# Eight of eleven FFN down projections of a decoder layer as seven half-size products, with the gated rows kept in device memory

## Chip, cores and metric

One core of a Trainium2 chip runs one program. The metric is the device time in microseconds (us); lower is better. Engines: PE (TensorE matmul, PEld its weight load), DVE (VectorE), ACT (ScalarE), POOL (GpSimd), SP (SyncE, which issues the transfers).

## The reference, cut to what matters

One step of a hybrid decoder layer on 1024 prompt tokens and 32 new ones (1056 columns): a half-step SwiGLU FFN, a mixer with attention and convolution, a cross-attention, and a second half-step FFN. The change concerns only the two FFNs:

```
def swiglu_ffn(x, g, w_gate, w_up, w_down):
    h = rmsnorm(x, g)
    return (jax.nn.silu(h @ w_gate) * (h @ w_up)) @ w_down
...
xp = xp + 0.5 * swiglu_ffn(xp, ffn1_norm[l], ffn1_w_gate[l], ffn1_w_up[l], ffn1_w_down[l])
```

D_MODEL is 1024, D_FF 2816, everything is float32.

## The kernel before

The tokens lie along the free dimension. T = 1056 columns; halves HW = 528, quarters QW = 264, thirds TT = 352. The residual stream `x_res` (8 blocks of 128 features by 1056) stays in SBUF. Every float32 product is three matmuls: high weight by high operand, high by low, low by high, where the high part is a rounded copy (ACT writes it) and the low part what remains (POOL for weights, DVE for operands).

`SevenFFN` computes one FFN. The 2816 hidden features are 22 chunks of 128, two chunks to a group, 11 groups. Group 0 (`plain`) multiplies directly. In each of the groups 1 to 10 a chunk's gate and up products are made by a seven-product scheme: seven "units" (gate1, gate2, T3, T2, T1, T4, up2), each 2 x 4 x 3 = 24 matmuls of 264 columns, so 168 matmuls to a chunk. The weight sums T1 to T4 are made on POOL (`summed`), the high parts on ACT (`sum_high`, `direct_high`), the low parts on POOL (`weight_low`), in six rotating buffers ("homes"). DVE evicts (`evict`), ACT does SiLU. The gated rows go to `f_ghi` and `f_glo`, and the group's down projection follows at once: 24 tiles (8 feature blocks by 3 thirds), each 2 chunks x 3 = 6 matmuls of 352 columns (lines 1271, 1275, 1276), each tile added to `x_res` by one DVE instruction (line 1553). Groups 2 to 9 are a hardware loop.

Every engine has its own in-order list. PE's `free` names what must be read before a PSUM bank is written again. In the last group DVE has more to do: in FFN1 (`nth == 0`) each add is followed by the low part of the next norm's operand (line 746), and `closing` on DVE releases PE's next product; in FFN2 ACT squares and scales each added tile and DVE sums the squares (line 714, and line 1588 for the last six tiles, one after the other), before the final normalisation and output.

Of the kernel before, what the change touches and what calls it, by code (L numbers as in the profile page):

```python
# [25 lines left out]
P = 128  # L26
# [49 lines left out]
FF_UNITS = 18 * (FF_CHUNKS // 2)  # L76
FF_LEAD = 6
FF_LOADS = 3 * (FF_CHUNKS // 2)
# [85 lines left out]
def hybrid_layer(nc, a, o):  # L164

    ctx = ExitStack()
    with ctx:
# [69 lines left out]
        for n, name in enumerate(("A22", "A11", "S3", "A21", "A12", "S1", "S2")):  # L237
# [16 lines left out]
                     rs=f_rs[:, :].rearrange("p (a b) -> p a b", a=NTT))  # L254
        conv_w0 = at("conv_w0", [P, 4, CONV_WIDTH], f_g_off + 16 * T + 12 * QW)
# [773 lines left out]
        class SevenFFN:  # L1029
# [24 lines left out]
            N_EV, N_ACT, N_MM = len(EVENTS), len(ACTS), 14  # L1054

# [9 lines left out]
            EV0, ACT0, MM0 = PLAIN_EV - 2 * N_EV, PLAIN_ACT - 2 * N_ACT, PLAIN_MM - 2 * N_MM  # L1065
            TOTAL_EV, TOTAL_ACT, TOTAL_MM = 2 * GROUPS * N_EV + EV0, 2 * GROUPS * N_ACT + ACT0, 2 * GROUPS * N_MM + MM0
# [28 lines left out]
            def done(self):  # L1095
                return self.tile_added(self.GROUPS - 1, self.N_TILES - 1)

            def event(self, g, c, name):
                return self.evicted, self.nth * self.TOTAL_EV + self.EV0 + self.N_EV * (2 * g + c) + self.EVENTS.index(name) + 1

            def act_done(self, g, c, name):
                return self.acted, self.nth * self.TOTAL_ACT + self.ACT0 + self.N_ACT * (2 * g + c) + self.ACTS.index(name) + 1
# [4 lines left out]
            def low_done(self, g, c, unit):  # L1107
                return past(self.low, self.UNITS * g + 7 * c + self.LOW_AT[unit])

            def high_done(self, g, c, unit):  # L1110
                return past(self.high, self.UNITS * g + 7 * c + self.HIGH_AT[unit])

            def sum_done(self, g, c, unit):
                return self.summed, 8 * (self.GROUPS - 1) * self.nth + 8 * (g - 1) + 4 * c + self.SUM_AT[unit]

            def down_unit(self, view, g, n):
                return past(view, self.UNITS * g + 15 + n)

            def tile_added(self, g, i):
                return self.added, self.N_TILES * (self.GROUPS * self.nth + g) + i + 1  # L1120

            def tile_done(self, g, i):
                return self.down_done, self.N_TILES * (self.GROUPS * self.nth + g) + i + 1

            def raw_landed(self, slot, g, n):
                return w_landed[slot], 16 * (self.landed0 + 3 * g + n + 1)

            def home_free(self, eng, g, n):

                eng.wait_ge(*past(self.used, self.UNITS * g + n - 4))  # L1130

            @staticmethod
            def home(c, unit):
                return (7 * c + unit) % HOMES
# [6 lines left out]
            def groups(self, eng, plain, group):  # L1141
# [16 lines left out]
            def loads(self, sp):  # L1158
# [5 lines left out]

                def group(g, first, last):
                    for c in range(2):
                        sp.wait_ge(*(self.sum_done(g, 0, self.W_T4) if c else self.down_unit(self.low, g - 1, 1)))
                        self.gate_load(sp, 2 * g + c)
                        sp.wait_ge(*(self.low_done(g, 0, self.UP2) if c else self.down_unit(self.low, g - 1, 3)))
                        self.up_load(sp, 2 * g + c)  # L1170
# [4 lines left out]
                self.groups(sp, plain, group)  # L1175
# [23 lines left out]
            def pe(self, pe, opening, closing=None):  # L1199
# [4 lines left out]
                def chunk(g, c, first):  # L1204
                    def free(unit, s):
                        if unit == self.GATE1:
                            return self.event(g, 0, "up_first%d" % s) if c else self.tile_added(g - 1, 18 + s)
# [2504 lines left out]
```

## Time and profile before

| | |
|---|---|
| median of 3 runs | 2503.03 us (2502.71 to 2507.26) |
| profiled execution: span, first to last instruction | 2501.9 us |
| what lies around the span (median less span) | 1.1 us |
| PE busy | 2448.5 us, 98% |
| DVE, POOL, ACT busy | 1348.7, 936.2, 911.0 us |
| DMA | 185.73 MB, mean 74 GB/s |

No time of its own is listed for the profiled execution beside its span. Busy is the share of time in which an engine had an instruction under way; matmuls overlap, so the sum of their durations is more than PE's busy time, and the distance from one to the next says what one costs.

### The profile page before, as it was taken

The page shows a single profiled execution, that of the slowest core. Times are in us where ns is not written, and L with a number is a line of the kernel's source. Part 1 is how long each engine was busy: PE and PEld are TensorE (multiplying, and loading weights), DVE is VectorE, ACT ScalarE, POOL GpSimd, SP SyncE. Part 2 cuts the span into 40 slices and gives each one's busy share as a digit, 9 for nine tenths or more (in the row PEclk, how much of TensorE's full clock was granted, in tenths as well). Part 3 has the DMA queues.
Part 4 walks back from the last instruction along what each step waited for, and adds up shares of the span by engine and source line. Part 5 has one row for each costly group of instructions (what it writes and reads, how often), then busy time and mean ns, then how long its engine had stood idle before and what let it go on. Part 6 is the DMA issues. An engine that isn't in the chain of part 4 may idle for free.

```text
span 2501.9 us, 47597 instructions
## 1 busy us (share of the span) xinstructions
PE 2448.5 (98%) x18207; PEld 2300.7 (92%) x18207; DVE 1348.7 (54%) x2603; ACT 911.0 (36%) x2042; POOL 936.2 (37%) x709
## 2 busy tenths in 40 slices
PE   7999999999999999998999999999999999999998
PEld 7999999999999998666777999789999999999998
DVE  6644444444474556765777761444654444444446
ACT  7333333333241334555443330332433233333326
POOL 2755555555543250002120222013465555555551
PEclk9999999999999999999999999999999999999999
DMA  3111111111123122006563312331111111111112
GB/s 124 34 52 51 50 50 50 50 50 50 51 70 117 49 67 80 1 1 261 186 230 127 130 42 74 130 126 43 43 52 52 51 50 48 45 46 46 50 51 87
DMA packets 175514, 185.73 MB, mean 74 GB/s; under 512 B 8360, under 2 KB 151049, under 8 KB 172566
## 3 DMA queue, kind: packets, MB, share of 16 engines
q1 hardware_dynamic: 171263, 144.55, 18.7%
q0 software_dynamic: 3584, 37.75, 3.8%
q8 instruction: 88, 1.44, 0.2%
q10 hardware_dynamic: 543, 1.69, 0.2%
q14 instruction: 36, 0.29, 0.0%
HBM read 167.66 MB, written 12.52 MB: 72 GB/s over the span
## 4 chain that ended last, share of the span: by engine, by line
PE 63%; ACT 3%; DVE 1%; issue 1%; ACTq 0%; DVEq 0%
PE ps L1236 5%; PE ps L1231 5%; PE ps L1235 5%; PE ps L397 5%; PE ps L400 5%; PE ps L401 5%; PE ps L1276 3%; PE ps L1275 3%; PE ps L1271 3%; PE ps L2352 2%; PE ps L2322 2%; PE ps L2367 1%; PE ps L2334 1%; PE ps L2533 1%; PE ps L2463 1%; PE ps L2664 1%
## 5 line engine op out<-in xcount | busy, mean ns | idle before, releaser
L1231 PE MATMUL ps<-op_hi_S,home_hi 128*128 128x264 f32 x1280 | 364.5, 285 | 0.0
L1235 PE MATMUL ps<-op_lo_S,home_hi 128*128 128x264 f32 x1280 | 364.0, 284 | 0.0
L1236 PE MATMUL ps<-op_hi_S,home_lo 128*128 128x264 f32 x1280 | 363.9, 284 | 0.0
L1553 DVE SCALAR_TENSOR_TENSOR x_res<-ps,x_res 128x352 f32<-128x352 f32 x528 | 270.4, 521 | 168.7 <-PE ps L1276 168.5
L1276 PE MATMUL ps<-f_ghi,home_lo 128*128 128x352 f32 x1056 | 340.8, 323 | 0.0
L1275 PE MATMUL ps<-f_glo,home_hi 128*128 128x352 f32 x1056 | 339.9, 322 | 0.0
L1271 PE MATMUL ps<-f_ghi,home_hi 128*128 128x352 f32 x1056 | 339.4, 321 | 0.4 <-DVE f_glo L1512 0.4
L1512 DVE TENSOR_TENSOR ps<-f_copy,ps 128x264 f32<-128x264 f32 x160 | 70.0, 438 | 456.5 <-PE ps L1236 456.5
L1231 PE MATMUL ps<-op_hi_A,home_hi 128*128 128x264 f32 x960 | 273.5, 285 | 0.0
L1236 PE MATMUL ps<-op_hi_A,home_lo 128*128 128x264 f32 x960 | 273.1, 284 | 0.0
L1235 PE MATMUL ps<-op_lo_A,home_hi 128*128 128x264 f32 x960 | 272.8, 284 | 0.0
L1236 PEld LDWEIGHTS ps<-op_hi_S,home_lo 128*128 128x128 f32 x1280 | 241.1, 188 | 0.0
L1235 PEld LDWEIGHTS ps<-op_lo_S,home_hi 128*128 128x128 f32 x1280 | 241.1, 188 | 0.0
L1231 PEld LDWEIGHTS ps<-op_hi_S,home_hi 128*128 128x128 f32 x1280 | 240.3, 188 | 0.0
L397 PE MATMUL ps<-h_hi,w_hi 128*128 128x352 f32 x696 | 229.5, 330 | 5.5 <-DVEq L3188 2.9
L1598 POOL TENSOR_TENSOR home_lo<-home_v,home_hi 128x512 fp32r<-128x512 f32 x160 | 205.2, 1293 | 68.3 <-ACT home_hi L1319 68.3
L400 PE MATMUL ps<-h_lo,w_hi 128*128 128x352 f32 x696 | 225.3, 324 | 0.0
L401 PE MATMUL ps<-h_hi,w_lo 128*128 128x352 f32 x696 | 225.2, 324 | 0.0
L2011 POOL CAST w_hi<-w_raw 128x1024 fp32r<-128x1024 f32 x40 | 41.9, 1048 | 484.6 <-PE ps L397 174.9
L1319 ACT ACTIVATE home_hi<-home_v 128x512 fp32r<-128x512 f32 x160 | 100.8, 630 | 310.9 <-POOL home_v L1611 309.6
L1598 POOL TENSOR_TENSOR home_lo<-f_raw,home_hi 128x512 fp32r<-128x512 f32 x120 | 156.7, 1320 | 124.9 <-ACT home_hi L1319 124.9
L1271 PEld LDWEIGHTS ps<-f_ghi,home_hi 128*128 128x128 f32 x1056 | 198.5, 188 | 0.9 <-DVE f_glo L1512 0.9
(394 smaller groups left out, 5698.6 us busy)
## 6 DMA issues: line engine op xcount, KB each, us to landing
f_raw<-in_ffn_w_gate SPq DMA_DIRECT2D x44, 512.0 KB, 3.8
f_raw<-in_ffn_w_up SPq DMA_DIRECT2D x44, 512.0 KB, 3.8
f_raw<-in_ffn_w_down SPq DMA_DIRECT2D x44, 512.0 KB, 3.7
ring<-in_cache_mem_k SPq DMA_DIRECT2D x16, 512.0 KB, 3.7
ring<-in_cache_mem_v SPq DMA_DIRECT2D x16, 512.0 KB, 5.0
w_raw<-in_w_in SPq DMA_DIRECT2D x14, 512.0 KB, 3.9
x_keep<-x_res SPq DMA_DIRECT2D x1, 4224.0 KB, 18.0
x_res<-x_keep SPq DMA_DIRECT2D x2, 2112.0 KB, 8.2
```

Source lines behind the costliest of these rows:

```text
L397: mm = pe.matmul(out, w_hi[:, slot, c0:c0 + m], hi, start=start, stop=False)
L400: pe.matmul(out, w_hi[:, slot, c0:c0 + m], lo, start=False, stop=False)
L401: return pe.matmul(out, w_lo[:, slot, c0:c0 + m], hi, start=False, stop=stop)
L1231: mm = pe.matmul(out, w, xhi[:, k, q], start=self.STARTS[unit] and k == 0, stop=False, skip_group_check=True)
L1235: pe.matmul(out, w, xlo[:, k, q], start=False, stop=False, skip_group_check=True)
L1236: mm = pe.matmul(out, lo, xhi[:, k, q], start=False, stop=self.STOPS[unit] and k == KH - 1, skip_group_check=True)
L1271: mm = pe.matmul(out, whi, f_ghi[:, c, cols], start=(c == 0), stop=False)
L1275: pe.matmul(out, whi, f_glo[:, c, cols], start=False, stop=False)
L1276: mm = pe.matmul(out, wlo, f_ghi[:, c, cols], start=False, stop=(c == 1))
L1319: act.activation(home_hi[h][:, :], src[:, :], ACT.Copy).then_inc(self.high[0], 1)
L1553: dve.scalar_tensor_tensor(out=x, in0=ps[:, bank, 0:TT], scalar=0.5, in1=x, op0=ALU.mult, op1=ALU.add).then_inc(self.added, 1)
L1598: pool.tensor_tensor(home_lo[h][:, :], src[:, :], home_hi[h][:, :].bitcast(F32), ALU.subtract).then_inc(self.low[0], 1)
```

## The change

Groups 0, 1 and 10 keep their direct down projection; group 10's now comes at the very end. Groups 2 to 9 are "staged": gate and up as before, but the gated rows are not projected. DVE writes them into a buffer `st` and forms four sums of 528 columns (S3 after the first chunk; S1, S2, S4 after the second, all three in a row), and SP stores 2 and then 5 planes of 528 columns to the device memory tensor `g_keep`. There are seven homes while groups are staged.

After group 10's gate and up, four "spans" run, each for two staged groups (K: two chunks each; tokens: two halves). A span has seven products; a product is 8 tiles of 264 columns (4 feature blocks by 2 quarters), each 2 x 3 = 6 matmuls: 336 matmuls. Its operands are read back from `g_keep` (seven transfers), split by ACT (`operand_high`) and DVE (`operand_low`, both inputs in SBUF); the 14 weight blocks, 8 of them sums, are made as before on POOL and ACT. DVE adds each tile to a running sum in SBUF (`span_sum`) or straight to `x_res`. After the last span POOL forms U2, U3, U4, V (16 additions of 528 columns, `combine`) and DVE adds them to `x_res` in 16 additions of 528 columns (`half_added`, both inputs in SBUF), twelve of them ahead of the tiles of group 10's down projection.

```
-FF_UNITS = 18 * (FF_CHUNKS // 2)
+STAGED = (2, FF_CHUNKS // 2 - 1)
+SPANS = 4
...
+        st = at("st", [P, 5, HW], f_g_off)
+        st_copy = at("st_copy", [P, 2, QW], f_g_off + 20 * HW)
...
+        g_keep = nc.dram_tensor("g_keep", (P, FF_CHUNKS // 2, 7, HW), F32, kind="Internal").ap()
...
                 plain()
                 group(1, True, False)
-                with eng.Fori(2, self.GROUPS - 1) as g:
-                    group(g, False, False)
-                group(self.GROUPS - 1, False, True)
+                with eng.Fori(*STAGED) as g:
+                    staged(g)
+                group(self.LAST, False, True)
+                if span is None:
+                    return
+                span(0)
+                with eng.Fori(1, SPANS - 1) as q:
+                    span(q)
+                span(SPANS - 1)
...
+                def staged(g):          # on SP
+                    chunk_after(g, 0, 2 * g + 1)
+                    sp.wait_ge(*self.event(g, 0, "S3"))
+                    sp.wait_ge(const_in, 32)
+                    sp.dma_start(g_keep[:, bass.ds(g, 1), 0:2, :], st[:, 1:3, :].unsqueeze(1)).then_inc(self.stored, 16)
+                    chunk_after(g, 1, 2 * g + 2)
+                    sp.wait_ge(*self.event(g, 1, "S4"))
+                    sp.wait_ge(const_in, 32)
+                    sp.dma_start(g_keep[:, bass.ds(g, 1), 2:7, :], st[:, :, :].unsqueeze(1)).then_inc(self.stored, 16)
...
                 def group(g, first, last):   # on ACT
+                    if last:
+                        act.wait_ge(*self.all_stored())
                     chunk(g, 0, first, last)
                     chunk(g, 1, first, last)
...
+                    for p in range(7):       # span, on PE
+                        pe.wait_ge(*self.operand_at(self.operand_low, q, p))
+                        for j in range(8):
+                            mb, cols = j // 2, slice(j % 2 * QW, (j % 2 + 1) * QW)
+                            out = ps[:, self.SPAN_BANKS[j], 0:QW]
+                            pe.wait_ge(*bank_free(p, j))
+                            for i in range(2):
+                                m = 2 * p + i
+                                if j == 0:
+                                    pe.wait_ge(*self.span_low(q, m))
+                                whi, wlo = (x[m % 7][:, mb * P:(mb + 1) * P] for x in (span_hi, span_lo))
+                                xhi, xlo = (x[p][:, i, cols] for x in (g_hi, g_lo))
+                                mm = pe.matmul(out, whi, xhi, start=(i == 0), stop=False)
...
+                                pe.matmul(out, whi, xlo, start=False, stop=False)
+                                mm = pe.matmul(out, wlo, xhi, start=False, stop=(i == 1))
...
+                def operand_low(q, p):   # on DVE
+                    dve.wait_ge(*self.operand_at(self.operand_split, q, p))
+                    dve.tensor_tensor(g_lo[p][:, :, :], g_v[p][:, :, :], g_hi[p][:, :, :].bitcast(F32),
+                                      ALU.subtract).then_inc(self.operand_low, 1)
...
+                    if c == 0:               # staged_end, on DVE
+                        evict("S3", st[:, 2, :], st[:, 1, :], st[:, 0, :], ALU.subtract, self.event(g, 0, "gated_first1"))
+                    else:
+                        evict("S1", st[:, 0, :], st[:, 0, :], st[:, 2, :], ALU.add, self.event(g, 1, "gated_first1"))
+                        evict("S2", st[:, 1, :], st[:, 1, :], st[:, 0, :], ALU.subtract, self.event(g, 1, "S1"))
+                        evict("S4", st[:, 4, :], st[:, 3, :], st[:, 1, :], ALU.add, self.event(g, 1, "S2"))
...
+                def plane_recombined(mb):
+                    if mb < 4:
+                        half_added(block_of(mb, 1), span_sum[3][mb][:, :], self.combined("U3", mb), self.span_tile(self.added, SPANS - 1, 3, 7))
+                        dve.wait_ge(*self.recombined(4 + mb))
+                    else:
+                        half_added(block_of(mb, 0), span_sum[0][mb - 4][:, :], self.combined("U4", mb - 4),
+                                   self.span_tile(self.added, SPANS - 1, 6, 7))
+                        half_added(block_of(mb, 1), span_sum[1][mb - 4][:, :], self.combined("V", mb - 4))
+                        dve.wait_ge(*self.recombined(8 + 2 * (mb - 4) + 1))
...
                 def down_add(g, i, mb, tt, bank):
+                    if g == self.LAST and tt == 0:
+                        plane_recombined(mb)
                     dve.wait_ge(*self.tile_done(g, i))
```

The words "on SP", "on ACT", "on PE" and "on DVE" behind some lines are added here. `span_free` lets the buffer of weight block m be written once PE has begun block m - 5, which for the odd block of product p is the start of product p - 2.

## Rows read from the trace of the kernel before

**Rows 1.** The page: busy time of each engine, and the granted clock.
```profile
PE 2448.5 (98%) x18207; PEld 2300.7 (92%) x18207; DVE 1348.7 (54%) x2603; ACT 911.0 (36%) x2042; POOL 936.2 (37%) x709
...
PEclk9999999999999999999999999999999999999999
```

**Rows 2.** Groups of PE by shape, and one FFN1 group as a window.
```profile
L1231 PE MATMUL ps<-op_hi_S,home_hi 128*128 128x264 f32 x1280 | 364.5, 285 | 0.0
...
L1276 PE MATMUL ps<-f_ghi,home_lo 128*128 128x352 f32 x1056 | 340.8, 323 | 0.0
...
200.70:264.60 63.90, 63.90 (x482) 63.90 (x481) 29.62 (x69) 19.82 (x46) 33.25 (x26) 1.00 0.17 50
```

**Rows 3.** Timeline of DVE: start, us, instruction; the first eviction of three chunks.
```profile
169.16 0.44 DVE L1512 TENSOR_TENSOR ps<-f_copy,ps 128x264 f32<-128x264 f32 x1 [4.08 <-PE ps L1236]
...
170.94 0.77 DVE L1512 TENSOR_TENSOR ps<-ps,f_rs 128x264 f32<-128x264 f32 x2
...
189.56 0.44 DVE L1512 TENSOR_TENSOR ps<-f_copy,ps 128x264 f32<-128x264 f32 x1 [2.54 <-PE ps L1236]
...
233.04 0.44 DVE L1512 TENSOR_TENSOR ps<-f_copy,ps 128x264 f32<-128x264 f32 x1 [4.05 <-PE ps L1236]
```

**Rows 4.** Timelines of POOL, ACT and DVE around a second chunk's start.
```profile
249.18 1.30 POOL L1611 TENSOR_TENSOR home_v<-f_raw 128x512 f32<-128x512 f32 x1
...
253.21 1.29 POOL L1598 TENSOR_TENSOR home_lo<-home_v,home_hi 128x512 fp32r<-128x512 f32 x1
...
251.90 0.63 ACT L1319 ACTIVATE home_hi<-home_v 128x512 fp32r<-128x512 f32 x1 [0.76 <-POOL home_v L1611]
...
248.91 0.44 DVE L1512 TENSOR_TENSOR ps<-ps,f_rs 128x264 f32<-128x264 f32 x1
```

**Rows 5.** Instructions on `op_v_S` (min/median/max ns), two timeline rows, one DVE group.
```profile
L836 DVE SCALAR_TENSOR_TENSOR op_v_S<-x_res,gains,op_v_S x32: 755/1421/1864, 47.8 to 1829.2; 128x528 f32<-128x528 f32 x32
...
L857 POOL TENSOR_TENSOR op_lo_S<-op_v_S,op_hi_S x24: 1322/1334/1806, 59.8 to 1831.8; 128x528 fp32r<-128x528 f32 x24
...
59.54 6.04 DVE L836 SCALAR_TENSOR_TENSOR op_v_S<-x_res,gains,op_v_S 128x528 f32<-128x528 f32 x4
...
59.77 7.00 POOL L857 TENSOR_TENSOR op_lo_S<-op_v_S,op_hi_S 128x528 fp32r<-128x528 f32 x4 [1.86 <-ACT op_hi_S L833]
...
L1512 DVE TENSOR_TENSOR f_glo<-ps,f_ghi 128x264 fp32r<-128x264 f32 x64 | 24.6, 426 | 2.1
```

**Rows 6.** Transfers: issues, KB each, us from issue to landing.
```profile
x_keep<-x_res SPq DMA_DIRECT2D x1, 4224.0 KB, 18.0
...
out<-kv_stage SPq DMA_DIRECT2D x1, 1024.0 KB, 5.1
```

**Rows 7.** Timelines of DVE and PE at the end of FFN1, and a window.
```profile
719.45 1.48 DVE L1553 SCALAR_TENSOR_TENSOR x_res<-ps,x_res 128x352 f32<-128x352 f32 x3 [0.84 <-PE ps L1276]
...
730.87 0.51 DVE L1553 SCALAR_TENSOR_TENSOR x_res<-ps,x_res 128x352 f32<-128x352 f32 x1
731.31 0.57 DVE L746 SCALAR_TENSOR_TENSOR h_lo<-x_res,gains,h_hi 128x352 fp32r<-128x352 f32 x1
731.80 0.51 DVE L1553 SCALAR_TENSOR_TENSOR x_res<-ps,x_res 128x352 f32<-128x352 f32 x1
...
736.33 2.28 DVE L746 SCALAR_TENSOR_TENSOR h_lo<-x_res,gains,h_hi 128x352 fp32r<-128x352 f32 x1
...
742.91 0.40 PE L397 MATMUL ps<-h_hi,w_hi 128*128 128x352 f32 x1 [2.91 <-DVEq L3188]
...
743.64:747.05 3.41, 3.41 (x13) 3.41 (x13) 3.41 (x2) 0.90 (x3) 3.33 (x2) 0.51 1.04 280
```

**Rows 8.** Timelines of DVE and ACT at the end of FFN2.
```profile
2460.10 1.39 DVE L1553 SCALAR_TENSOR_TENSOR x_res<-ps,x_res 128x352 f32<-128x352 f32 x3
...
2462.83 1.37 DVE L1553 SCALAR_TENSOR_TENSOR x_res<-ps,x_res 128x352 f32<-128x352 f32 x3
...
2482.61 0.53 DVE L1588 TENSOR_TENSOR acc_end<-acc_end,sq_end 128x352 f32<-128x352 f32 x1 [0.69 <-ACT sq_end L1451]
```

More of the change, by code:

```diff
@@ L1177, in plain_products, with span_low, span_high, span_free @@
+                self.groups(sp, plain, group, staged)
+                for q in range(SPANS):
+                    span(q)
+            def span_low(self, q, m):
+                return past(self.low, self.span_unit(q) + m + 1)
+            def span_high(self, q, m):
+                return past(self.high, self.span_unit(q) + m + 1)
+            def span_free(self, eng, q, m):
+                eng.wait_ge(*past(self.used, self.span_unit(q) + m - 4))
             def plain_products(self, pe, c, u, q, free=None, planes=range(KH), starts_unit=False):
@@ L1649, in group, with staged, span_low @@
                     chunk(g, 1)
-                    for n in range(4):
-                        down_low(g, n)
                     if not last:
+                        for n in range(4):
+                            down_low(g, n)
                         ahead(g + 1, 0)
-                self.groups(pool, plain, group)
+                def staged(g):
+                    chunk(g, 0)
+                    ahead(g, 1)
+                    chunk(g, 1)
+                    ahead(g + 1, 0)
+                def span_low(q, m):
+                    name, i = self.SPAN_WEIGHTS[m // 2], m % 2
+                    src = span_v[m % 7][:, :] if name[0] == "T" else block(i, name)
+                    pool.wait_ge(*self.span_high(q, m))
+                    pool.tensor_tensor(span_lo[m % 7][:, :], src, span_hi[m % 7][:, :].bitcast(F32), ALU.subtract).then_inc(self.low[0], 1)
@@ new lines, in block, with span_sum_of @@
+                def block(i, name):
+                    r, h = int(name[1]) - 1, int(name[2]) - 1
+                    return span_raw[i][:, r, 512 * h:512 * h + 512]
+                def span_sum_of(q, i, name, a, b, op, *waits):
+                    m = 2 * self.SPAN_WEIGHTS.index(name) + i
+                    for known, value in waits:
+                        pool.wait_ge(known, value)
+                    self.span_free(pool, q, m)
+                    pool.tensor_tensor(span_v[m % 7][:, :], a, b, op).then_inc(self.summed, 1)
@@ new lines, in combine @@
+                def combine(name, mb, out, a, b, *waits):
+                    for known, value in waits:
+                        pool.wait_ge(known, value)
+                    pool.tensor_tensor(span_sum[out][mb][:, :], span_sum[a][mb][:, :], span_sum[b][mb][:, :], ALU.add).then_inc(self.summed, 1)
+                self.groups(pool, plain, group, staged, span)
+                at = [self.span_tile(self.added, SPANS - 1, p, 7) for p in range(7)]
+                for mb in range(4):
+                    combine("U2", mb, 2, 2, 0, at[2])
@@ L1879, in _ @@
                 if m < 2:
-                    sp.wait_ge(w_used, U_WIN - 4 + m)
-                    sp.wait_ge(*ffn1.down_unit(ffn1.low, ffn1.GROUPS - 1, 1 + 2 * m))
+                    sp.wait_ge(w_used, U_WIN - 3)
+                    sp.wait_ge(*ffn1.down_unit(ffn1.low, ffn1.LAST, 1 + 2 * m))
                 else:
```

420 lines of the change are left out of this document (360 added, 60 removed).

## The prediction

> **What bounds the kernel now.** I read the page first: PE is busy 98% of the span, at full granted clock in all slices, while DVE, ACT and POOL are busy 36 to 54% [rows 1]. In one FFN1 group (window) PE is busy in all 63.90 us, DVE in 29.6 and POOL in 33.3 [rows 2]. So what the groups cost is what PE issues. The durations of matmuls overlap, so I take the price of one from distances. Between the first evictions of a group's two chunks lie 20.40 us, and between those of two groups 63.88 us [rows 3]. A chunk is 168 matmuls of 264 columns: 121.4 ns each. Two chunks leave 23.08 us for the down projection, 144 matmuls of 352 columns: 160.3 ns each. PE waits for nobody inside a group. The exceptions are the two ends. At the end of FFN1 PE sits idle 2.91 us until DVE releases it, and then runs 3.41 us at half clock (0.51, the 1.2 GHz level) before it is at 2.4 GHz again [rows 7]. At the end of FFN2 DVE and ACT hand the last tiles to each other while PE waits [rows 8].
>
> **Matmuls.** Removed: the down projections of 8 groups in each of 2 FFNs, 16 x 23.08 = 369.3 us. Added: 8 spans of 336 matmuls of 264 columns. Each tile has 6 matmuls and one wait, as before, and this shape has its price in the row above: 336 x 121.4 ns = 40.8 us, in all 326.4. Net -42.9 us. The six matmuls of a tile write one bank in both forms, and weights are loaded for each matmul in both, so I take the shape's price as it is. Were the unequal fixed part mispriced by 2 ns a matmul, it would be 5 us; I take nothing.
>
> **Staged groups.** PE now goes from chunk to chunk with no down projection between. The step from a group's first to its second chunk is that already, and it runs at 20.4 us without a PE wait [rows 2, 3]. POOL has 11 instructions of 1.3 us (14 us) to a chunk. In the second chunk (PE starts it at 249.1, which is 36 matmuls before the eviction that follows, and its fourth product T2 at 257.8) POOL finishes the low part for T2 at 254.5: 3.3 us early [rows 4]. New in this stretch are four DVE sums of 528 columns. The nearest row is 755 ns alone, but in the stretch where POOL works without pause four such take 6.04 us, 1.5 to 1.8 us each, and POOL's own go from 1.33 to 1.75 us [rows 5]. DVE instructions with an input in PSUM stay at 426 ns with POOL busy. So a DVE instruction with both inputs in SBUF and one of POOL take turns. The Trainium skill, "SBUF — State Buffer", section on two separate sides, says the pair of ports that DVE and GpSimd share is an exclusive lock held for a whole instruction; the trace agrees in kind. By that rule alone a pair would take 0.69 + 1.33 = 2.02 us and the sum would be 1.2 us higher; the rows have 1.75. It speaks against this change, which adds two-input SBUF work on DVE everywhere. Here three sums cost POOL 1.3 us of its 3.3: hidden. Stores of 528 KB and 1320 KB per group and loads of 2 MB are far under what DMA moves (4224 KB in 18.0 us [rows 6]), and a second chunk's gated rows need the buffer 12 us after the store: hidden.
>
> **The wait of the last group.** ACT may not begin group 10 before the last store has landed. Let PE start group 10 at 0. DVE's last eviction of group 9 before the sums starts at -0.1 (as 248.91 to 249.1 [rows 4]); two more evictions, then S1, S2, S4 beside POOL's three sums at 1.5 each: done at 5.5 (3.6 if they take 0.75). The store of 1320 KB lies between 1024 KB at 5.1 us and 4224 KB at 18.0 [rows 6]: 6.0 us (5.2 to 7.5). ACT is free at 11.7, makes the high parts of T1 and T2 (1.1), POOL the low part of T2 (1.3): 14.2. PE wants it at 72 x 121.4 ns = 8.7. Stall 5.5 us, with bounds 2.7 and 8. Queued behind ACT's wait are its copies of the first product, late by as much, but nothing else lands on PE after T2. S4 at 3.6 and 5.2 for the store give the first bound, S4 at 6.5 and 7.5 the second. The clock: 2.91 us of idling were followed by 3.41 us at half speed, which is 1.7 us lost [rows 7]; the same here. 7.2 us per FFN, 14.4 in all. Bounds 5 (2.7 each and no fall of the clock) and 19.
>
> **Entry to the spans.** DVE's first two `operand_low` (1056 columns, about 1.3 us alone, twice the 528 row) stand before four evictions of the last chunk, so the banks of the span's first tiles come free about 0.5 us late: 1.0 in all, bounds 0 and 4. In exchange the down projection of group 10 no longer waits for its own evictions.
>
> **Inside the spans.** Per product PE has 5.83 us. DVE has 8 tile additions, at 0.34 us from start to start (two evictions in 0.77 [rows 3]), and one `operand_low` of 1.3 plus up to 1.3 for POOL's instruction before it: 4.1 to 5.4. POOL has 22 instructions for 7 products, 4.0 us, plus up to 1.1 lent to DVE: 5.1. Both under PE, but POOL may fill a block only two products ahead. The tightest chain is T3's second block: its sum may start when T2 starts; sum, two low parts and one loan are 1.4 + 2.5 + 1.2 = 5.1, and behind a backlog from T4 it comes 0.3 us late. I take 0.3 per span, 2.4 in all; bounds 0 and 16 (2 us a span, where every loan falls into such a chain).
>
> **The two ends.** In FFN1 DVE is already the bound of the last down projection: two adds with a low part between are 0.93 us apart (730.87 to 731.80), a tile takes PE 0.96, and the closing comes 26.4 us after PE's start [rows 7]. In FFN2 DVE needs 2.73 us for three tiles (2460.10 to 2462.83) against PE's 2.88, and its last six are a chain over ACT [rows 8]. The change puts twelve additions of 528 columns in this list: 12 x 0.69 (755 ns less an overlap of 0.07) = 8.3, plus eight waits of DVE on its own result (no row of this stretch has one: 0 to 0.2 each, taken at 0.1); minus the first, which falls before the first tile is there (0.8), minus 0.5 for the earlier start: 7.8. Beside that POOL makes U4 and V, eight of 1.33 us, from about 2 us into this stretch, and takes turns with DVE's low parts and sums. One POOL instruction of 2.56 us made one of DVE's last 2.28 in place of 0.57 [rows 7]. About six meet a busy DVE and cost 0.5 each: 3.0. 10.8 us per FFN, 21.6 in all. Bounds per FFN: 7 (no turns) and 14 (all eight at 0.8 to 0.9). In FFN1 the whole of it is waiting before the mixer's products, as the 2.9 us were.
>
> **Sum.** -42.9 + 14.4 + 1.0 + 2.4 + 21.6 = -3.5 us. Span 2501.9 becomes 2498.4; the median of the runs lies 1.1 above the span, so 2499.5 us.
>
> **Rivals.**
> (a) *The new waits are short.* The store is nearly hidden (S4 at 3.6, landing in 5.2: 4.4 us per FFN with the clock) and POOL's turns cost nothing at the ends (7 per FFN): -42.9 + 8.8 + 14 + 0 = -20, so 2483. For it: ACT's and DVE's ordinary rows are short, and the turns show only in few places. Against: the turns are in the rows wherever both work.
> (b) *DVE and POOL bound the spans* (the other side): where loan and residual reach 2 us in each product instead of 1.2, POOL's chain for T4 and T3 comes 1.5 to 2 us late in every span: 8 x 1.8 = 14 more, so about 2514. It decides from 1.3 us of delay per product on. For it: in rows 5 POOL's instructions lengthen by 0.4 for every DVE instruction of half the size. Against: POOL pauses some 30% of the time in a span (22 x 1.3 us of 40.8).
> (c) *The short matmuls don't save*: if the spans' matmuls ran at the price of the long ones less the columns at 2.4 GHz (160.3 - 36.7 = 123.6 ns) the spans cost 332.2 and the gain is 37: 2505.
>
> **How the numbers follow.** The forecast, 2499.5 with its own range 2493 to 2506, 0.40; (a) 0.25; (b) 0.25; (c) 0.05; something unlisted 0.05. The terms' bounds give -42.9 + 5 + 14 = -24 and -42.9 + 19 + 4 + 16 + 28 = +24; 8 in 10 is 2481 to 2517. A difference under 0.2% (5 us) can't be told from none here. Faster than 2498: (a) and 0.4 of the forecast, 0.42. Within: half of the forecast, (c) and a part of (b), 0.31. Slower than 2508: 0.27.
>
> **What would show it.** In the trace after: spans of 40.8 us with no PE idle (they are right if the first tiles of successive spans lie under 41.2 us apart); matmuls of the span 121 ns apart; a hole of some 5 us in PE, followed by half clock, three products into group 10 of each FFN, with ACT behind it and a 1320 KB transfer of 6 us; DVE without a pause through the last down projections, each ending 9 to 12 us later than before, PE's idle before L397 about 10 us; DVE instructions with two SBUF inputs at 1.3 to 2.5 us where POOL works. The prediction is wrong if ACT's wait is over before PE needs T2, if POOL's low parts come late in each product of a span, or if the second half of FFN1's or FFN2's end is not DVE's.

## The result

| | before | after |
|---|---|---|
| median, same chip | 2503.91 us (2502.71 to 2507.26, 4 runs) | 2531.11 us (2521.03 to 2538.81, 4 runs) |
| ratio | | 1.0104, 95% interval 1.0076 to 1.0132 |
| span of the profiled execution | 2501.9 us | 2536.7 us (time 2538.81) |
| mean granted clock | 0.994 | 0.982 |

The change makes the kernel 1.0% slower. The forecast was 2499.5 us with a range of 2481 to 2517, so it was wrong: the measured time lies 14 us above that range. The page after, busy time and granted clock:

```profile
PE 2433.2 (96%) x18591; PEld 2280.7 (90%) x18591; DVE 1511.1 (60%) x2691; ACT 953.0 (38%) x2018; POOL 1175.4 (46%) x853
...
PEclk9999999999989999999999999999999999999998
```

Against [rows 1] PE is busy 15.3 us less, though the span is 34.8 us longer: PE waits. PE's longest waits say for whom (releaser, us in total, times, longest):

```profile
PE ps L1468 <- DVE x_res L1930: 20.7, 5, 6.5
PE ps L1426 <- POOL home_lo L1982: 10.7, 2, 5.4
PE ps L1533 <- DVE span_sum L1921: 9.6, 2, 4.8
PE ps L421 <- DVEq L3635: 9.0, 1, 9.0
```

The second is the wait of the last group, and was foreseen. The other three are DVE's. FFN1 after by stage, as windows: groups 2 to 10, the four spans, the last down projection with what follows it. Columns: busy us of PE, PEld, DVE, ACT, POOL, then granted clock, DMA share, GB/s:

```profile
164.90:541.60 376.70, 371.02 (x3027) 370.57 (x3025) 172.93 (x357) 134.46 (x308) 261.92 (x197) 0.99 0.32 99
541.60:715.00 173.40, 168.45 (x1344) 167.66 (x1345) 142.65 (x264) 61.80 (x89) 135.57 (x94) 0.98 0.39 118
715.00:759.33 44.33, 26.40 (x146) 24.96 (x145) 43.70 (x58) 13.46 (x24) 17.37 (x13) 0.83 0.09 24
```

In the last window DVE is busy 43.70 of 44.33 us: DVE is the bound, as [rows 7] had it, but the 26.5 us that this stretch took before have become 44.3, where the prediction has 37.3. The timeline of DVE and of POOL there (start, us):

```profile
715.55 13.14 DVE L1881 SCALAR_TENSOR_TENSOR x_res<-span_sum,x_res 128x528 f32<-128x528 f32 x1
728.73 1.39 DVE L1930 SCALAR_TENSOR_TENSOR x_res<-ps,x_res 128x352 f32<-128x352 f32 x3
...
730.53 0.70 DVE L1881 SCALAR_TENSOR_TENSOR x_res<-span_sum,x_res 128x528 f32<-128x528 f32 x1
```
```profile
715.39 2.57 POOL L1986 TENSOR_TENSOR home_lo<-f_raw,home_hi 128x512 fp32r<-128x512 f32 x2
717.91 10.22 POOL L2087 TENSOR_TENSOR span_sum<-span_sum,span_sum 128x528 f32<-128x528 f32 x8
```

One half-add, 0.70 us when alone, takes 13.14 us. It begins while POOL starts a row of ten instructions, two low parts and the eight sums U4 and V, and ends 0.56 us after the row does. POOL's instructions are not lengthened: 2.57 us for two and 10.22 for eight. DVE gets no turn in the row at all; this is called a hold from here on. PE fills its eight banks and stops:

```profile
722.52 0.32 PE L1473 MATMUL ps<-f_ghi,home_lo 128*128 128x352 f32 x1
729.31 0.66 PE L1468 MATMUL ps<-f_ghi,home_hi 128*128 128x352 f32 x1 [6.47 <-DVE x_res L1930]
...
759.33 0.63 PE L421 MATMUL ps<-h_hi,w_hi 128*128 128x352 f32 x1 [9.00 <-DVEq L3635]
```

In the second FFN the half-add takes 11.85 us. The same happens in the first span of each FFN, to DVE's split of one operand. DVE's row, then PE's next matmul, 5.09 us behind the start of its last one, then POOL's row beside them; DVE asked while POOL's second low part ran, and got in behind the seventh, so six stood in its way:

```profile
559.66 8.14 DVE L1800 TENSOR_TENSOR g_lo<-g_v,g_hi 128x1056 fp32r<-128x1056 f32 x1 [1.42 <-ACT g_hi L1624]
...
568.20 0.59 PE L1533 MATMUL ps<-g_hi,home_hi 128*128 128x264 f32 x1 [4.81 <-DVE span_sum L1921]
```
```profile
557.94 5.05 POOL L2049 TENSOR_TENSOR home_lo<-home_v,home_hi 128x512 fp32r<-128x512 f32 x4
562.95 1.30 POOL L2049 TENSOR_TENSOR home_lo<-f_raw,home_hi 128x512 fp32r<-128x512 f32 x1
564.20 1.26 POOL L2049 TENSOR_TENSOR span_lo<-span_raw,span_hi 128x512 fp32r<-128x512 f32 x1
565.42 1.26 POOL L2049 TENSOR_TENSOR home_lo<-f_raw,home_hi 128x512 fp32r<-128x512 f32 x1
```

The usual time of each of the two DVE instructions, as min/median/max in ns, shows how rare this is: 54 of the 56 splits were over within 2.5 us, most of them with POOL working beside them.

```profile
L1881 DVE SCALAR_TENSOR_TENSOR x_res<-span_sum,x_res x32: 694/700/13144, 682.4 to 2513.1; 128x528 f32<-128x528 f32 x32
L1800 DVE TENSOR_TENSOR g_lo<-g_v,g_hi x56: 1240/1892/8140, 536.5 to 2459.3; 128x1056 fp32r<-128x1056 f32 x56
```

Windows around the wait of the last group and around the end of FFN1 show that PE's idling costs the clock too. PE idles for 5.4 us up to 506.06; from 505.4 the clock is 0.50, the 1.2 GHz level, for 6.8 us. Behind the last down projection, where PE waited often and then idled 9.0 us, it is 0.50 for 13.6 us. In [rows 7] it was 3.41 us after 2.91.

```profile
500.40:505.40 5.00, 0.28 (x3) 0.07 (x1) 0.37 (x2) 1.88 (x5) 0.66 (x1) 1.00 0.80 223
505.40:512.20 6.80, 6.13 (x28) 6.14 (x29) 1.09 (x4) 2.54 (x8) 4.33 (x4) 0.50 0.26 77
512.20:515.60 3.40, 3.40 (x30) 3.40 (x30) 1.11 (x3) 1.26 (x3) 2.58 (x3) 1.00 0.00 0
...
751.10:764.70 13.60, 5.37 (x18) 5.40 (x19) 13.16 (x23) 5.45 (x11) 3.76 (x2) 0.50 0.35 94
```

### The profile page after: what moved, and what is told of

Its sections match the earlier page's. It is cut to its first block, busy times and chain, and to the rows that moved or that the text cites. A ratio compares the mean times of both kernels' runs of the same rounds, so it can differ in the third digit from the quotient of the medians.

```text
span 2536.7 us, 48654 instructions
## 1 busy us (share of the span) xinstructions
PE 2433.2 (96%) x18591; PEld 2280.7 (90%) x18591; DVE 1511.1 (60%) x2691; ACT 953.0 (38%) x2018; POOL 1175.4 (46%) x853
## 4 chain that ended last, share of the span: by engine, by line
PE 55%; DVE 4%; ACT 3%; issue 1%; POOL 0%; DMA 0%; ACTq 0%; DVEq 0%; SPq 0%
PE ps L1426 5%; PE ps L1431 5%; PE ps L1430 5%; PE ps L424 4%; PE ps L421 4%; PE ps L425 4%; PE ps L2799 2%; PE ps L1533 2%; PE ps L1537 2%; PE ps L1536 2%; PE ps L2769 2%; PE ps L2814 1%; PE ps L2781 1%; PE ps L2980 1%; PE ps L2910 1%
## 5 line engine op out<-in xcount | busy, mean ns | idle before, releaser
L1815 DVE TENSOR_TENSOR ps<-st_copy,ps 128x264 f32<-128x264 f32 x192 | 83.8, 436 | 319.2 <-PE ps L1431 279.8
L1982 POOL TENSOR_TENSOR home_lo<-home_v,home_hi 128x512 fp32r<-128x512 f32 x160 | 211.2, 1331 | 92.7 <-ACT home_hi L1553 92.7
L1533 PE MATMUL ps<-g_hi,home_hi 128*128 128x264 f32 x768 | 223.9, 292 | 10.3 <-DVE span_sum L1921 9.6
L1536 PE MATMUL ps<-g_lo,home_hi 128*128 128x264 f32 x768 | 220.3, 287 | 0.0
L1537 PE MATMUL ps<-g_hi,home_lo 128*128 128x264 f32 x768 | 219.7, 286 | 0.0
L1431 PEld LDWEIGHTS ps<-op_hi_A,home_lo 128*128 128x128 f32 x960 | 180.9, 188 | 0.0
L1430 PEld LDWEIGHTS ps<-op_lo_A,home_hi 128*128 128x128 f32 x960 | 180.9, 188 | 0.0
L1426 PEld LDWEIGHTS ps<-op_hi_A,home_hi 128*128 128x128 f32 x960 | 180.3, 188 | 0.0
```

The lines of the kernel that those rows point to most:

```text
L1426: mm = pe.matmul(out, w, xhi[:, k, q], start=self.STARTS[unit] and k == 0, stop=False, skip_group_check=True)
L1430: pe.matmul(out, w, xlo[:, k, q], start=False, stop=False, skip_group_check=True)
L1431: mm = pe.matmul(out, lo, xhi[:, k, q], start=False, stop=self.STOPS[unit] and k == KH - 1, skip_group_check=True)
L1533: mm = pe.matmul(out, whi, xhi, start=(i == 0), stop=False)
L1536: pe.matmul(out, whi, xlo, start=False, stop=False)
L1537: mm = pe.matmul(out, wlo, xhi, start=False, stop=(i == 1))
```

## The experiments

Two theories went in. Theory 1: DVE, with two inputs in SBUF, is shut out for as long as POOL issues one ready instruction straight after the other. Theory 2: DVE simply has too much work at the ends. A third, in e1, was that the stores or the clock by themselves are what costs. All kernels are edits of the changed kernel; e3, e4 and e10 leave work out, the others compute everything. They ran on several chips, on which the kernel before took 2503.9 to 2507.5 us, so rows are compared by their ratios. Stages are read from each trace, first matmul to first matmul, in us, as FFN1 / FFN2; the last column of FFN2 runs to the end of the kernel.

| kernel | median | ratio to before, same chip | groups 2 to 10 | spans | last down |
|---|---|---|---|---|---|
| before | 2503.91 | 1 | | | 26.5 / 45.2 |
| after | 2531.11 | 1.0104 | 376.7 / 375.4 | 173.4 / 173.0 | 44.3 / 63.3 |
| e1 rows broken | 2517.59 | 1.0047 [1.0029, 1.0064] | 375.1 / 375.9 | 166.2 / 166.2 | 41.1 / 62.1 |
| e2 store wait later | 2529.20 | 1.0105 [1.0069, 1.0141] | 373.2 / 373.3 | 166.1 / 166.1 | 44.4 / 65.0 |
| e3 short combines | 2512.25 | 1.0019 [1.0005, 1.0033] | 375.6 / 376.4 | 173.1 / 166.1 | 33.9 / 54.7 |
| e4 short half-adds | 2512.35 | 1.0028 [1.0009, 1.0046] | 376.6 / 377.4 | 177.5 / 166.0 | 36.6 / 56.9 |
| e5 satisfied waits | 2524.06 | 1.0075 [1.0058, 1.0091] | 377.3 / 376.2 | 173.1 / 166.0 | 44.3 / 64.3 |
| e6 store wait at copy 7 | 2520.10 | 1.0070 [1.0052, 1.0088] | 369.7 / 370.8 | 166.0 / 172.2 | 44.4 / 65.1 |
| e7 e1 + early half-adds | 2514.43 | 1.0038 [1.0024, 1.0052] | 376.6 / 376.4 | 167.0 / 167.0 | 37.6 / 58.6 |
| e8 e6 + e7 | 2499.86 | 0.9984 [0.9974, 0.9993] | 370.6 / 370.6 | 167.0 / 167.0 | 37.6 / 58.6 |
| e9 one pause | 2521.37 | 1.0059 [1.0037, 1.0081] | 376.1 / 376.5 | 167.4 / 165.9 | 43.0 / 62.1 |
| e10 no recombination | 2476.12 | 0.9884 [0.9867, 0.9900] | 369.6 / 370.5 | 166.2 / 166.2 | 27.6 / 46.6 |
| e11 e8 without U4 and V | 2496.95 | 0.9962 [0.9949, 0.9976] | 372.1 / 369.5 | 170.0 / 169.6 | 35.0 / 53.7 |

**e1, rows broken.** POOL waits for its own last result at each step.

```
                     pool.wait_ge(*self.span_high(q, m))
+                    if m >= 6:
+                        pool.wait_ge(*self.span_low(q, m - 1))
...
+                    if (name, mb) in self.COMBOS[1:]:
+                        pool.wait_ge(*self.combined(*self.COMBOS[self.COMBOS.index((name, mb)) - 1]))
+                    if mb == 0 and name in ("U3", "U4"):
+                        pool.wait_ge(*self.down_unit(self.low, self.LAST, 1 if name == "U3" else 3))
                     pool.tensor_tensor(span_sum[out][mb][:, :], span_sum[a][mb][:, :], span_sum[b][mb][:, :], ALU.add).then_inc(self.summed, 1)
```

> Nothing is left out; only POOL's own program gets waits on results that it has itself just made: each low part of a span from the seventh on waits for the one before it, and each sum of the recombination for the instruction before it, so that POOL's rows of ready instructions get a gap after each one. Theory 1 (a DVE instruction with two inputs in on-chip memory is shut out for as long as POOL issues one ready instruction straight after the other): the 8.14 us operand split of span 0 and the 13.14 and 11.85 us first half-adds fall to 3 us or less, TensorE's gaps at 563 us (5.1 us), 722 us (6.8 us) and their images in the second FFN go, and with the slow clock behind them the time falls by 25 to 45 us against the changed kernel. Theory 2 (DVE has simply too much to do at the ends): the first half-add gets short, but the gaps are only moved, and the time falls by less than 10 us. Theory 3 (what costs is the traffic to device memory or the clock by itself): no change, within 5 us.

The two instructions in question, now:

```profile
L1881 DVE SCALAR_TENSOR_TENSOR x_res<-span_sum,x_res x32: 696/708/2846, 672.7 to 2487.2; 128x528 f32<-128x528 f32 x32
L1800 DVE TENSOR_TENSOR g_lo<-g_v,g_hi x56: 1248/1848/2373, 534.2 to 2436.2; 128x1056 fp32r<-128x1056 f32 x56
```

The long ones are gone, and with them 7.2 and 6.8 us of the spans. But the last down projections are only 3.2 and 1.2 us shorter, and the kernel stands 0.47% above before instead of 1.04%, which is 14 us: less than the 25 that theory 1 gave and more than the 10 of theory 2 or the 5 of the third. The first two are half right: the hold is real, but at the ends POOL's sums cost DVE nearly as much when they take turns.

**e5, the control.** Waits at the same places, on a count reached long before (the span's first weight sum), so no pause.

> The control to the broken rows: POOL gets a wait at each of the same places, but on a count that was reached long before (the first weight sum of the span), so that the row gets the same instructions and no pause. Nothing is left out. If what matters is the pause of 0.17 us in which POOL holds nothing ready, the first half-adds stay at 11 to 14 us, TensorE's gap of 6.8 us behind them stays, and the time is that of the changed kernel, 2520 to 2540 us. If a waiting instruction of any kind is enough to let DVE in, it is that of the broken rows, 2514 to 2521 us.

```profile
715.10 13.07 DVE L1881 SCALAR_TENSOR_TENSOR x_res<-span_sum,x_res 128x528 f32<-128x528 f32 x1
```
```profile
714.87 2.57 POOL L1986 TENSOR_TENSOR home_lo<-f_raw,home_hi 128x512 fp32r<-128x512 f32 x2
717.38 10.22 POOL L2093 TENSOR_TENSOR span_sum<-span_sum,span_sum 128x528 f32<-128x528 f32 x8
```

As in the changed kernel, to 0.1 us, and the time is in the range for "only the pause counts". A wait that is already satisfied did not let DVE in.

**e9, one pause.** V's first sum waits for U4's last, and the eleventh low part of a span for the tenth; nothing else.

> Nothing is left out; POOL gets a single pause in each row instead of one behind every instruction: the first V sum waits for the result of the last U4 sum, and the eleventh low part of a span for the tenth. Theory 1 in its exact form (DVE is let in at the first moment at which POOL has nothing ready, and not before): the first half-add of the first FFN, asked for at the second of the two low parts ahead of the U4 sums, is held for what is left of them and the four U4 sums, 1.3 x 5 to 6 and its own 0.7, that is 7 to 9 us instead of 13.1, and in the second FFN some 6 to 8 instead of 11.9; a held operand split is cut to under 5 us. The time lies between that of the changed kernel and that of the broken rows, 2515 to 2530 us. If DVE gets in after a fixed time or by chance, the half-add's time has nothing to do with the place of the pause.

```profile
708.57 8.31 DVE L1881 SCALAR_TENSOR_TENSOR x_res<-span_sum,x_res 128x528 f32<-128x528 f32 x1
```
```profile
708.57 2.59 POOL L1986 TENSOR_TENSOR home_lo<-f_raw,home_hi 128x512 fp32r<-128x512 f32 x2
711.10 5.20 POOL L2091 TENSOR_TENSOR span_sum<-span_sum,span_sum 128x528 f32<-128x528 f32 x4
716.47 6.16 POOL L2091 TENSOR_TENSOR span_sum<-span_sum,span_sum 128x528 f32<-128x528 f32 x4 [0.17 <-POOL span_sum L2091]
```

The half-add ends at 716.88, which is 0.58 us after the one pause of 0.17 us begins; in the changed kernel it ended 0.56 us after the whole row. It is 7.07 us in the second FFN and the longest split 4.46 us, all inside what the exact form of theory 1 gave. So where DVE is held, the place of the pause sets how long.

**e3 and e4, which of the two parties.** In e3 POOL's 16 sums, in e4 DVE's 16 half-adds touch 8 columns in place of 528.

```
+ e3: pool.tensor_tensor(span_sum[out][mb][:, 0:8], span_sum[a][mb][:, 0:8], span_sum[b][mb][:, 0:8], ALU.add)
+ e4: dve.scalar_tensor_tensor(out=out[:, 0:8], in0=x[:, 0:8], scalar=0.5, in1=out[:, 0:8], op0=ALU.mult, op1=ALU.add)
```

> Left out: the 16 sums on POOL that recombine the planes touch 8 of their 528 columns, so their result is not that of the reference; all waits stay. Theory 1: the row of eight sums at 717.9 us is gone, the first half-add takes 3 us or less instead of 13.1 and 11.9, and TensorE's gap at 722 us goes: about 10 us less per FFN and 3 to 7 of clock, 22 to 34 in all; the gap of span 0 at 563 us stays. Theory 2 (DVE's own work at the ends is too long): the last down projection stays near 40 us, the time falls by less than 10.

> Left out: the 16 half-adds on DVE touch 8 of their 528 columns, so their result is not that of the reference; all waits and POOL's full sums stay. Theory 1: the first half-add is still held for as long as POOL's row runs (over 8 us), since it is the two inputs that shut it out and not its length; the time falls only by the 0.6 us x 12 per FFN that the others lose, 8 to 15 us in all. Theory 2: the ends shrink by the whole of it, and the first half-add with them; over 20 us.

e4's first half-add:

```profile
718.87 10.81 DVE L1881 SCALAR_TENSOR_TENSOR x_res<-span_sum,x_res 128x8 f32<-128x8 f32 x1
```

A DVE instruction of 8 columns, 0.16 us elsewhere in this trace, takes 10.81 us: its length has nothing to do with it. e3 shortens FFN1's end by 10.5 us, to 33.9; what is left above the 26.5 of before is mostly the half-adds themselves. e4 shortens it by 7.7. In median e3 stands 0.85% and e4 0.76% under the changed kernel's ratio, 21 and 19 us: e3 just misses the 22 to 34 of theory 1, and e4 has more than its 8 to 15 but not the over 20 of theory 2, whose other condition (the end stays near 40 in e3) isn't met either. The hold itself went as theory 1 had it in both; e3's first half-add took 0.70 us.

**e2 and e6, the wait for the stores.** e2 puts ACT's wait behind the roundings of T1 and T2, e6 ahead of the copies of the T3 product.

```
 group:
-                    if last:
-                        act.wait_ge(*self.all_stored())
 chunk (e6):
+                    if last and c == 0:
+                        act.wait_ge(*self.all_stored())
                     for s in range(2):
                         act.wait_ge(*self.product_done(g, c, self.W_T3, s))
```

> Nothing is left out; ACT's wait for all stores, in the last group, stands behind the two weight roundings T1 and T2 instead of ahead of them, right before the first copy that overwrites the store's source. If the wait costs what the profile after shows (a gap of 5.66 and 5.63 us, and then 6.83 us at half clock, that is 3.4 us lost, in each FFN), the two gaps go and the time falls by about 18 us against the changed kernel, 11 of it the gaps and 7 the clock. If the half clock behind it has another cause, about 11. If the store itself is what is late (its landing, 13 us after the last staged instruction), the copies come late instead, the second W products wait, and the gain is under 5.

> Nothing is left out; ACT's wait for all stores stands one step later still, ahead of the two copies of the second product bank (the copies of the first bank touch no byte that is being stored). The store lands at 503.1 us of the trace with the wait ahead of the first copies, some 3.7 us after TensorE ran dry; the second copies are needed 5.9 us later. So the gap goes in both FFNs: against the changed kernel 5.6 us per FFN and the 3.4 us that the half clock behind it costs, 18 us in all; against the kernel with the wait ahead of the first copies 3.6 and up to 3.4 per FFN, 7 to 14. If the half clock comes from something else, 11 and 7. The DVE instructions that POOL's rows hold at the ends stay as long as they were.

ACT in e2 and then in e6, in the last group:

```profile
502.58 0.67 ACT L1638 ACTIVATE f_copy<-ps 128x264 f32<-128x264 f32 x2 [7.60 <-DMA g_keep<-st]
```
```profile
495.75 0.66 ACT L1636 ACTIVATE f_copy<-ps 128x264 f32<-128x264 f32 x2
...
503.67 0.67 ACT L1643 ACTIVATE f_copy<-ps 128x264 f32<-128x264 f32 x2 [6.10 <-DMA g_keep<-st]
```

e2 misses its first two branches and hits the third: PE's hole only falls from 5.66 to 3.67 us, since the landing is what is late, and the median gains nothing. e6 leaves 1.55 us of it. Against the changed kernel groups 2 to 10 get 7.0 and 4.7 us shorter, 11.7 of the 18 expected, and the ratio falls by 0.34%, or 8.5 us, less than either branch gave. Against e2 it falls by 0.35%, 8.8 us, inside the 7 to 14 given, but the same stages fall by only 6.1 us, so that part of it is luck: the executions of e2 spread over 26 us, and the spans differ by held splits, which are there in one execution and not in another. The held half-adds stayed as they were, 13.18 and 11.95 us.

**e7 and e8, early half-adds, and all three.** U2's sums stand between the last low parts of the last span, U3's half-adds in its last plane:

```
+                            if last and p == 6 and j % 2:
+                                half_added(block_of(mb, 1), span_sum[3][mb][:, :], self.combined("U3", mb))
...
+                        if isinstance(q, int) and q == SPANS - 1 and m >= 10:
+                            combine("U2", m - 10, 2, 2, 0, self.span_tile(self.added, SPANS - 1, 2, 7))
                         span_low(q, m)
```

> Nothing is left out; POOL's rows are broken as before, its first four sums are made between the last low parts of the last span, and the four half-adds of U3 run in the last plane of that span, where DVE is idle 0.30 us of every 0.74, so that eight half-adds and not twelve lie on DVE's way through the last down projection. DVE's way there is then 24 x (0.44 + 0.49) + 8 x 0.66 = 27.6 us with no turns and some 32 with them, against 41.1 us with the rows broken alone: 7 to 13 us less per FFN in the first, less in the second, and 10 to 22 us against the broken rows in all. If POOL's sums take as many turns from DVE as before wherever they stand, only the 2.6 us of the four half-adds go, 5 us in all.

> Nothing is left out; broken rows, early sums and half-adds, and the wait for the stores ahead of the second copies, together. If the three causes are separate and are what took the 42.9 us of saved matmuls: 2517.6 (rows broken) less 18 for the stores and 10 to 22 for the ends, 2478 to 2490 us, 0.7 to 1.2% faster than the kernel before. If the clock or the traffic eats what is freed, 2500 or more.

The ends fall by 3.5 and 3.4 us against e1, not by 7 to 13, and each FFN's spans pay 0.8 us for it; by the ratio e7 gets 2 us and not 10 to 22. That is e7's other branch, in which POOL's sums take as many turns wherever they stand: 5 us, and the stages give 5.3. DVE is still slow in the last down projection because of POOL's U4 and V, now with pauses. e8's DVE in the last down projection, beside them and behind them:

```profile
714.68 0.51 DVE L1931 SCALAR_TENSOR_TENSOR x_res<-ps,x_res 128x352 f32<-128x352 f32 x1
715.12 1.22 DVE L770 SCALAR_TENSOR_TENSOR h_lo<-x_res,gains,h_hi 128x352 fp32r<-128x352 f32 x1
...
724.51 0.52 DVE L1931 SCALAR_TENSOR_TENSOR x_res<-ps,x_res 128x352 f32<-128x352 f32 x1
724.95 0.57 DVE L770 SCALAR_TENSOR_TENSOR h_lo<-x_res,gains,h_hi 128x352 fp32r<-128x352 f32 x1
```

Tile additions read one input in PSUM and take 0.51 either way; the split h_lo, two inputs in SBUF, takes 1.22 instead of 0.57. e8 as a whole missed its 2478 to 2490 and all but meets its other branch, 2500 or more. Against e1 the later wait for the stores gave 4.5 and 5.3 us in groups 2 to 10, not 18, and the ends gave 6.9, not 10 to 22. With 0.9984 it is the first that beats the kernel before, by 4 us.

**e10, what the matmuls are worth.** e1, e3, e4 and e6 together.

> Left out: the sums of the recombination on POOL and the half-adds on DVE touch 8 of their 528 columns, so the result is not that of the reference. POOL's rows are broken and the stores' wait stands ahead of the second copies. It shows what the matmul arithmetic is worth with the three costs taken away: the kernel before less 42.9 us, plus what remains for the entry and the inside of the spans (1.7 us per FFN by the prediction), 2462 to 2470 us. If the seven half-size products save less than their count of matmuls says, or the traffic to device memory slows TensorE, it stays above 2480.

2476.12: 29.3 us under before on the same chip, where 35 to 43 were expected; it lies between its two branches. FFN1 in windows:

```profile
164.30:533.90 369.60, 368.27 (x3026) 367.81 (x3024) 172.77 (x357) 134.72 (x308) 262.42 (x197) 1.00 0.33 101
533.90:700.20 166.30, 165.97 (x1345) 165.32 (x1346) 132.88 (x264) 61.73 (x89) 132.55 (x104) 1.00 0.40 123
700.20:727.70 27.50, 23.13 (x145) 22.84 (x145) 24.98 (x58) 13.46 (x24) 3.60 (x2) 0.98 0.15 39
```

**e11, without the second sums.** On e8: U4 and V are not formed; DVE adds half of the T1 plane into both of its targets in planes 3 to 5 of the last span, and half of U2 and U3 in the last down projection.

```
+                T1_AT = {(3, 1): 0, (3, 5): 1, (4, 1): 2, (4, 5): 3, (5, 1): 4, (5, 3): 5, (5, 5): 6, (5, 7): 7}
...
+                            if last and (p, j) in T1_AT:
+                                n = T1_AT[p, j]
+                                half_added(block_of(4 + n // 2, n % 2), span_sum[1][n // 2][:, :], self.span_tile(self.added, SPANS - 1, 1, 7))
```

> Nothing is left out; on top of broken rows, the early sums and half-adds and the late wait for the stores, POOL's eight second sums (U4 and V) are gone: DVE adds half of the T1 plane straight into both of its targets, eight half-adds in the planes 3 to 5 of the last span, and half of U2 and U3 in the last down projection, eight half-adds there as before. POOL then has no two-input sum while the last down projection runs, and h_lo's splits, 1.22 us each next to those sums, take 0.57. DVE's way through the last down projection, 37.6 us from its start to the closing stage in the kernel with all three edits, falls to 28 to 32 us (24 x (0.44 + 0.49) + 8 x 0.66 = 27.6 and its start), 5 to 9 us per FFN in the first and less in the second: 2487 to 2495 us, against 2499.9. If the eight half-adds overfill the last span (8 x 0.43 + 2 to 4 x 0.66 and a split of 1.9 against 5.9 us a plane), the gain is given back there, and it stays at 2497 or above.

2496.95, ratio 0.9962 [0.9949, 0.9976]: the fastest kernel here that computes everything. The time lies just under the second branch. The ends are 2.7 and 4.9 us shorter than e8's, and 3.0 and 2.6 are given back in the spans, as the last sentence of the expectation feared.

e11 also shows where theory 1 stops. Around the end of FFN1's last span POOL makes four low parts in a row with no pause, all of them ready since 703.68 us. DVE's half-adds beside them are not held; each gets in behind one POOL instruction, and POOL's are lengthened from 1.3 to 1.7 us. POOL's row, then DVE's:

```profile
705.88 6.89 POOL L1994 TENSOR_TENSOR home_lo<-f_raw,home_hi 128x512 fp32r<-128x512 f32 x4
```
```profile
707.09 1.09 DVE L1881 SCALAR_TENSOR_TENSOR x_res<-span_sum,x_res 128x528 f32<-128x528 f32 x1
...
708.78 1.12 DVE L1881 SCALAR_TENSOR_TENSOR x_res<-span_sum,x_res 128x528 f32<-128x528 f32 x1
...
710.51 1.10 DVE L1881 SCALAR_TENSOR_TENSOR x_res<-span_sum,x_res 128x528 f32<-128x528 f32 x1
```

So a row without a pause can hold DVE, and need not.

## Why the prediction was wrong

The predicted and measured stages of the profiled execution, in us:

| step | predicted | measured |
|---|---|---|
| groups 2 to 10, with the wait of the last group and the entry | 367.2 + 7.2 + 0.5 = 374.9 each | 376.7 / 375.4 |
| four spans | 163.2 + 1.2 = 164.4 each | 173.4 / 173.0 |
| last down, FFN1 | 26.5 + 10.8 = 37.3 | 44.3 |
| last down to the end, FFN2 | 45.2 + 10.8 = 56.0 | 63.3 |

The excess is 2.3 + 17.6 + 7.0 + 7.3 = 34.2 us; 3.9 between the two FFNs and 0.6 at the start make 38.7. The forecast of the span, 2498.4, is missed by 38.3; the difference of 0.4 is rounding in the prices of the stages. The 3.9 are mostly the clock. In the stretch between the FFNs the changed kernel's trace has 19.1 us at the 1.2 GHz level, e4, e7 and e9 have 16.6 to 19.3, and these four need 1164.7 to 1165.9 us for it; e1, e2, e3, e5, e6, e8 and e11 have 10.9 to 12.0 us at that level and need 1162.0 to 1162.4. Less half of the time at 1.2 GHz all eleven need 1156.2 to 1156.6. The kernel before has 13.7 us at that level and needs 1155.0 beside half of it, so 2.7 of the 3.9 are the clock and 1.2 stay open.

- **Matmuls, -42.9 us: nearly right.** From span to span PE's first matmuls are 41.23 us apart (591.32, 632.55, 673.78 us of the trace after), where 40.8 + 0.3 was said: 122.7 ns a matmul, 1.3 more than inside a chunk, the same in e10. The price was taken from units that put 12 matmuls into a bank; a span's tile has 6, as only the old down projection had. Whether that is the 1.3 ns no run separates. The first span takes 1.3 us more than the others even where nothing is held (e10: 533.93 to 576.48 is 42.55). The rival *short matmuls don't save* had 123.6 ns, 2.2 more: at most six tenths of that came, 3.4 us in all. e10's profiled span is 27.8 us under before and not 42.9. The rest, 15.1 us, is 5.3 in groups 2 to 10 (1.5 of the stores' hole in each FFN among them), 6.0 in the spans, 1.1 and 1.5 at the ends and 1.2 between the FFNs.
- **The wait of the last group, 7.2 per FFN: right.** The hole was to be 5.5 us and is 5.66 and 5.63; the store of 1320 KB took 5.75 us, where 6.0 was said. Without any of it the stage takes 369.6 - 1.5 = 368.1 and 370.5 - 1.5 = 369.0 (e10), so the wait with its half clock cost 8.6 and 6.4. The clock's part was taken as 1.7 us. The low level lasts 6.8 us in both FFNs, but begins at the end of the idling in the first and halfway through it in the second, so that PE works for 6.2 us of it in one and 3.9 in the other: up to 3.1 and 1.9 us lost.
- **Entry to the spans: right.** The last matmul of group 10 and the first of the spans are 0.6 and 0.4 us apart in the trace after.
- **Inside the spans, 0.3 a span: the failed step, in part.** Three of four spans behave as predicted, to 0.1 us. In the first one of each FFN DVE was shut out by a row of six low parts, 8.14 us, and PE stood 5.09 us and then ran at half clock: 7.2 and 6.8 us (after less e1). The rival *DVE and POOL bound the spans* had the right parties and the wrong mechanism: no chain of loans in every product, but one block. Its 2514 is nearer to the result, yet does not reach it.
- **The two ends, 10.8 per FFN: the failed step.** Its sentence "takes turns with DVE's low parts and sums" and the term of 3.0 for it. The half-adds alone, predicted at 7.8, cost 33.9 - 27.6 = 6.3 in FFN1 (e3 less e10). POOL's sums beside them, predicted at 3.0, cost 44.33 - 33.87 = 10.5 without pauses (after less e3) and 41.1 - 33.9 = 7.2 with turns enforced (e1 less e3). So even where the turns are enforced the term was less than half of what it should have been, and at the first half-add there were no turns at all.

What I misread was the Trainium skill's rule together with [rows 5]. "SBUF — State Buffer" (section on two separate sides) says that whoever starts first gets the pair of ports for the whole instruction. In [rows 5] four DVE instructions and four of POOL alternate, and I took that for the general case. In the traces here the loser can be kept out for a whole row of the other's instructions (six, nine or ten of them), and e1, e5 and e9 show that a pause in the row ends it. What begins it is open. Without any pause DVE was let in behind a single POOL instruction in [rows 5], in e11's row above and at nearly all splits, but the first half-add of each FFN was held in all five kernels whose row of eight full sums has no pause (after, e2, e4, e5, e6: 9.6 to 13.2 us).

Where the 42.9 us went, then, in profiled times of both FFNs: 15.0 to the wait of the last group (12.0 after less e10, and the 3.0 that e10 keeps), 14.0 to the held splits (after less e1), 6.3 + 8.0 = 14.3 to the half-adds (e3 less e10), 10.5 + 8.6 = 19.1 to POOL's sums beside them (after less e3), and 6.0 to the spans' own length over 163.2 (e10). That is 68.4. The whole to be explained is 42.9 + 34.8 = 77.7, and the 9.3 left are 3.9 between the FFNs, 0.6 at the start, 2.3 more in groups 2 to 10 and 2.5 that the ends of e10 keep. The first four are differences between traces with and without the cause, so shown, but each is of one execution. Which executions hold a split is chance as far as the traces tell: of six profiled kernels with unbroken low rows (after, e2 to e6) two held two splits for 8 us, three held one and e2 none; of the five in which those low parts pause (e1, e7, e8, e10, e11) none held one there. e11 held one split for 4.90 us just ahead of the spans, beside three POOL instructions that do not pause in it either. Such chance would explain why the changed kernel spreads from 2521 to 2539 us, but only one of its executions has a trace.

## What to carry to other kernels

A VectorE instruction with two SBUF inputs can wait not for one GpSimd instruction but for a whole row of them. It does not always, and what decides is open here, so take the row as the bound: before work is put on either engine, count the longest row on GpSimd without a real pause, and check the slack on VectorE against that row. A wait of GpSimd on its own last result, 0.17 us each, cuts the row; a shorter VectorE instruction is held as long. And GpSimd sums beside a stage in which VectorE is already the bound cost it most of their time even when they take turns (7.2 of 10.2 us in FFN1): move them to a stage with room, or remove them.

## What was not expected of the hardware

- A VectorE instruction of 528 columns took 13.14 us beside ten GpSimd instructions, one of 8 columns 10.81 us beside nine, one of 1056 columns 8.14 us beside six; GpSimd's took 1.26 to 1.36 each, as alone.
- A satisfied wait between the GpSimd instructions changed nothing (13.07 us); one pause of 0.17 us ended the hold there (8.31 us).
- Beside another row of four ready GpSimd instructions without a pause the same VectorE instruction took 1.09 to 1.12 us, and GpSimd's 1.7 each: there the two took turns.
- VectorE's tile additions, with one input in PSUM, took 0.41 to 0.53 us whether GpSimd worked beside them or not.
- Around 5.4 us of idling TensorE was at 1.2 GHz for 6.8 us, with its matmuls 0.22 us apart instead of 0.12; behind the last down projection of FFN1, where it was busy about 6 of 9 us and then idle 9.0, the low level held for 13.6 us.
